# 192 instead of 160 gathered token slots in the last stage of a streaming encoder layer on one core

## What is computed

```
def block(args):
    xb, idb, gb = args
    h = jax.nn.gelu(jnp.einsum('td,thkd->thk', xb, u_table[idb]), approximate=False)
    w = (gb * h).astype(xb.dtype)
    return jnp.einsum('thk,thkd->td', w, v_table[idb]).astype(xb.dtype)
...
x = layer_norm(ALPHA * x + peer(x, peer_w_query, peer_sub_keys, peer_u, peer_v), ln2_g, ln2_b)
```

## Time and profile before

| what | value |
|---|---|
| median of 3 runs | 3592.86 us |
| the profiled execution | 3591.76 us |
| its span | 3590.0 us |
| TensorE (PE) busy | 3506.9 us, 98% |
| VectorE (DVE) busy | 2732.9 us, 76% |
| ScalarE (ACT) busy | 1186.2 us, 33% |
| GpSimd (POOL) busy | 1856.6 us, 52% |
| mean granted TensorE clock | 0.991 of full speed |

### The profile page before, as it was taken

One profiled execution on the slowest core, in us unless ns is written; L12 is line 12 of the kernel. 1 busy time (PEld: TensorE's weight loads), 2 busy tenths in 40 slices (PEclk: granted clock), 3 DMA queues, 4 the chain that ended last, 5 costly groups with the idle time before them and its releaser, 6 DMA issues. The chain is left out here.

```text
span 3590.0 us, 62687 instructions
## 1 busy us (share of the span) xinstructions
PE 3506.9 (98%) x25376; PEld 3461.0 (96%) x25376; DVE 2732.9 (76%) x3476; ACT 1186.2 (33%) x1155; POOL 1856.6 (52%) x1107
## 2 busy tenths in 40 slices
PE   8999999998999999999999999999999999999996
PEld 7999999898999999999999999999999999999996
DVE  4866858634899787777777777776688888888876
ACT  2332333413222234444444434443222222222224
POOL 3443434455444577868887870002665666664321
PEclk9999999999999999999999999999999999999998
DMA  4222222563225678888988897778799999898962
GB/s 153 74 76 77 82 73 71 201 276 132 83 94 165 201 208 228 220 228 226 228 219 229 225 229 217 230 224 288 277 354 351 351 360 361 343 361 351 356 259 99
DMA packets 466252, 788.24 MB, mean 220 GB/s; under 512 B 78976, under 2 KB 376384, under 8 KB 402384
## 3 DMA queue, kind: packets, MB, share of 16 engines
q1 hardware_dynamic: 337920, 547.99, 46.3%
q0 software_dynamic: 83840, 168.15, 14.7%
q10 hardware_dynamic: 44368, 70.57, 5.4%
HBM read 711.43 MB, written 209.34 MB: 256 GB/s over the span
## 5 line engine op out<-in xcount | busy, mean ns | idle before, releaser
L616 POOL TENSOR_TENSOR wl<-wraw,wh 128x512 fp32r<-128x512 f32 x352 | 539.9, 1564 | 686.5 <-ACT wh L1121 678.6
L667 POOL DMA_INDIRECT g_scratch<-picks,g_col x384 | 682.0, 1776 | 175.9 <-issue 149.4
L1121 ACT ACTIVATE wh<-wraw 128x2048 fp32r<-128x2048 f32 x216 | 414.0, 1917 | 970.2 <-PE ps L1037 740.4
L1037 PE MATMUL ps<-Wh,wh 128*128 128x384 f32 x2048 | 686.4, 335 | 7.6 <-DVE wl L2029 3.8
L1037 PE MATMUL ps<-Wh,wl 128*128 128x384 f32 x2048 | 684.8, 334 | 0.0
L1037 PE MATMUL ps<-Wl,wh 128*128 128x384 f32 x2048 | 684.8, 334 | 0.0
L1005 PE MATMUL ps<-xh,wl 128*128 128x272 f32 x1792 | 518.5, 289 | 0.0
L1005 PE MATMUL ps<-xl,wh 128*128 128x272 f32 x1792 | 515.5, 288 | 0.0
L1005 PE MATMUL ps<-xh,wh 128*128 128x272 f32 x1792 | 515.1, 287 | 0.3 <-DVE wl L1914 0.3
L707 PE MATMUL ps<-xh,wh 128*128 128x272 f32 x2304 | 490.1, 294 | 18.3 <-DVE ext L1671 11.9
L707 PE MATMUL ps<-xl,wh 128*128 128x272 f32 x2304 | 481.0, 290 | 0.0
(11 more groups left out here) (311 smaller groups left out, 6886.7 us busy)
## 6 DMA issues: line engine op xcount, KB each, us to landing
wraw<-in_u_t SPq DMA_DIRECT2D x128, 1024.0 KB
v_rows<-in_v_t SPq DMA_DIRECT2D x256, 512.0 KB
wraw<-in_v_t SPq DMA_DIRECT2D x128, 1024.0 KB
wraw<-in_w_in SPq DMA_DIRECT2D x40, 1024.0 KB
g_scratch<-zeros ACTq DMA_DIRECT2D x32, 768.0 KB, 7.7
h_scratch<-hb ACTq DMA_DIRECT2D x64, 384.0 KB
gt<-g_scratch SPq DMA_DIRECT2D x64, 384.0 KB
hg<-h_scratch SPq DMA_DIRECT2D x64, 384.0 KB
```

Source lines behind the costliest of these rows:

```text
L616: ins = nc.gpsimd.tensor_tensor(wl[:, u, part], wraw[:, u, part], f(wh[:, u, part]), ALU.subtract)
L667: nc.gpsimd.indirect_dma_start(g_elem, bass.IndirectOffsetOnAxis(ap=idx, axis=0), gate, None, compute_op=ALU.add).then_inc(g_put, 16)
L1037: ins = mat(out, w[:, u, d * EG + e], m[:, e], start=(begin and e == 0 and w is wh and m is Wh[v]), stop=(end and e == EG - 1 and w is wl))
L1121: go(wh[:, u], wraw[:, u], ACT.Copy).then_inc(whi, 1)
```

## The change

`TD` becomes 352. The dense way then has 352 tokens, and the gathered way 192: the last 128 as before and the 64 tokens 352 to 415, on 128 partitions as two parts of 64 (`NB` = 2), which take 64 slots. `ALL` becomes 192. They are spread over 116 tiles, 3 to 118, instead of 110. The GELU values are gathered 8 slots ahead instead of 32 (`HB`), and the weights are formed for 8 slots at a time. In `v_tile` the two blocks' products with `wh` come first, then both blocks' products with `wl`, and the wait for `wl` stands in front of these. The turning of `y_x` moves from behind tile 118 to behind tiles 120 and 122, in two halves, and its sum is added to `acc` in two halves inside the last group's loop. `fsum1`, `fsum2` and `fsq` move to the memory of the gather buffers.

```diff
-TD = 384
+TD = T - P - RT
-NGC = TD // GC
+NGC = -(-TD // GC)
-NB = P // TS
-XSLOTS = SLOTS // NB
+XSLOTS = -(-SLOTS // NB)
-HB = 32
+HB = 8
...
+RT, NB = 64, 2
...
             def v_tile(g, v, i, u):
 
+                pe.wait_ge(whi, (g * EG + (A_V + u + 1)) + i * 2)
+                pe.wait_ge(w_s, g * (EG // 2) + EG // 2)
+                outs = [v_out(i, u, d) for d in range(2)]
+                for d, (out, kept) in enumerate(outs):
+
+                    pe.wait_ge(y_add, g * KT + (i * 4 + (2 * u + d + 1)))
+                    begin = not kept or (isinstance(g, int) and g == 0)
+                    for e in range(EG):
+                        mat(out, wh[:, u, d * EG + e], Wh[v][:, e], start=(begin and e == 0), stop=False)
+                        mat(out, wh[:, u, d * EG + e], Wl[v][:, e], start=False, stop=False)
                 pe.wait_ge(dlo, (g * EG + (A_V + u + 1 - D0)) + i * 2)
-                pe.wait_ge(w_s, g * (EG // 2) + EG // 2)
-                for d in range(2):
-
-                    pe.wait_ge(y_add, g * KT + (i * 4 + (2 * u + d + 1)))
-                    out, kept = v_out(i, u, d)
+                for d, (out, kept) in enumerate(outs):
+                    end = not kept or (isinstance(g, int) and g == NG - 1)
                     for e in range(EG):
-                        ins = v_products(v, u, d, e, out, not kept or (isinstance(g, int) and g == 0),
-                                         not kept or (isinstance(g, int) and g == NG - 1))
+                        ins = mat(out, wl[:, u, d * EG + e], Wh[v][:, e], start=False, stop=(end and e == EG - 1))
                     ins.then_inc(mm, 1)
...
-                if m == EG - 2:
-                    pe.wait_ge(y_sp_u, 4)
+            for m in range(EG):
+                v_tile(NG - 1, 1, m // 2, m % 2)
+                if m in (0, 2):
+                    half = m // 2
+                    pe.wait_ge(y_sp_u, 4 + half)
                     pe.wait_ge(y_sp_s, 2)
-                    for k in range(KT):
-                        ins = mat(ps[:, TURN, k * TS:(k + 1) * TS], y_x[:, k * P:(k + 1) * P], fold[:],
+                    for j in range(HK):
+                        k = half * HK + j
+                        ins = mat(ps[:, TURN, j * RT:(j + 1) * RT], y_x[:, k * P:(k + 1) * P], fold[:],
                                   start=True, stop=True)
                     ins.then_inc(y_turn, 1)
-            v_group(NG - 1, 1)
...
-            STEP0, STEPS = EG, (NG - 1) * EG - EG - 2
+            STEP0, STEPS = 3, (NG - 1) * EG - 4
...
             for k in range(KT):
+                if k % HK == 0:
+                    v_.wait_ge(y_turn, 5 + k // HK)
+                    a_ = acc[:, k:k + HK, TD:T - P]
+                    C.done(stt_(a_, a_, ALPHA, ps[:, TURN, 0:HK * RT].rearrange("p (k t) -> p k t", k=HK),
+                                ALU.mult, ALU.add), y_sp_u)
                 add_y((NG - 1) * EG + k // 2, k % 2)
```

More of the change, by code:

```diff
@@ L265, in program @@
-        zeros = at("zeros", [P, 4, TD], F32, S0)
[L266 to L271, removed]
+        XB = XSLOTS * 4
+        x_ids, x_hid = [at(n, [P, XSLOTS], U32, S0 + 15520 + k * XB) for k, n in enumerate(("x_ids", "x_hid"))]
@@ L273, in program @@
+        s_ids = at("s_ids", [P, SLOTS], U32, S0 + o + 0 * SLOTS * 4)
+        s_hid = at("s_hid", [P, SLOTS], U32, S0 + o + 1 * SLOTS * 4)
+        s_gate = at("s_gate", [P, SLOTS], F32, S0 + o + 2 * SLOTS * 4)
+        s_h = at("s_h", [P, SLOTS], F32, S0 + o + 3 * SLOTS * 4)
+        s_w = at("s_w", [P, SLOTS], F32, S0 + o + 4 * SLOTS * 4)
+        s_tok = at("s_tok", [P, 1], F32, S0 + o + 5 * SLOTS * 4)
         hb = at("hb", [P, 2, 2, T], F32, M0)
-        Wh = [at(f"Wh{v}", [P, EG, TD], F32R, X0 + v * 2 * EG * ROWD) for v in range(2)]
@@ L275, in program @@
-        Wl = [at(f"Wl{v}", [P, EG, TD], F32R, X0 + v * 2 * EG * ROWD + EG * ROWD) for v in range(2)]
-        G0 = X0 + 4 * EG * ROWD
+        WROW = 384 * 4
+        Wh = [at(f"Wh{v}", [P, EG, 384], F32R, X0 + v * 2 * EG * WROW)[:, :, 0:TD] for v in range(2)]
+        Wl = [at(f"Wl{v}", [P, EG, 384], F32R, X0 + (v * 2 + 1) * EG * WROW)[:, :, 0:TD] for v in range(2)]
+        G0 = X0 + 4 * EG * WROW
         gath = [at(f"gath{v}", [P, D], F32, G0 + v * D * 4) for v in range(3)]
@@ L287, in program @@
         assert (EG + 2) * ROWD <= 15520
-        fsum1 = at("fsum1", [P, T], F32, M0)
-        fsum2 = at("fsum2", [P, T], F32, M0 + ROW)
-        fsq = [at(f"fsq{u}", [P, T], F32, M0 + (2 + u) * ROW) for u in range(2)]
+        fsum1 = at("fsum1", [P, T], F32, G0)
+        fsum2 = at("fsum2", [P, T], F32, G0 + ROW)
+        fsq = [at(f"fsq{u}", [P, T], F32, G0 + (2 + u) * ROW) for u in range(2)]
         XT = HK * TH * 4
@@ L361, in program @@
             sem("slots_done"), sem("slots_turned"), sem("turned_used"))
-        sh_in = [sem(f"slot_h_in{b}") for b in range(ALL // HB)]
+        sh_in = [sem(f"slot_h_in{b}") for b in range(2)]
+        assert ALL % HB == 0 and SLOTS % HB == 0
         sv_in = [sem(f"slot_v_in{b}") for b in range(3)]
@@ L676, in _ @@
                     for tt in G_TILES:
-                        put(g_idx[:, tt, c:c + 1], picks[:, 0, tt, h, k:k + 1])
+                        m = min(P, TD - TOPK_TILES[tt][0])
+                        put(g_idx[0:m, tt, c:c + 1], picks[0:m, 0, tt, h, k:k + 1])
             pool.wait_ge(ids_s, 1)
@@ L1877, in _ @@
             C.done(ts_(s_h[:], s_w[:], float(SD), s_tok[:], ALU.mult, ALU.add), dve)
-            C.done(ts_(s_h[:], s_h[:], float(TS), None, ALU.add), dve)
+            C.done(ts_(s_h[:], s_h[:], float(RT), None, ALU.add), dve)
             C.done(cp(s_hid[:], s_h[:]), dve)
             def rest(a):
-                return picks[0:TS, a, REST].rearrange("p h k -> p (h k)")
+                return picks[0:RT, a, REST].rearrange("p h k -> p (h k)")
             C.done(stt_(r_f[:], rest(1), float(P), rest(2), ALU.mult, ALU.add), dve)
             cp(r_ids[:], r_f[:])
-            C.done(ts_(r_f[:], r_f[:], float(SD), s_tok[0:TS], ALU.mult, ALU.add), dve)
+            C.done(ts_(r_f[:], r_f[:], float(SD), s_tok[0:RT], ALU.mult, ALU.add), dve)
             C.done(cp(r_hid[:], r_f[:]), dve)
[L1888 to L1891, removed]
+            for x in (x_ids, x_hid, x_gate):
+                C.done(nc.vector.memset(x[:], 0), dve)
+            C.done(tt_(fold[:], ident[:, 0:RT], ident[:, RT:2 * RT], ALU.add), ids_s)
             def flat(a):
@@ L2105, in _ @@
                     slot(s)
-            v_.wait_ge(y_turn, 5)
-            a_ = acc[:, :, TD:T - P]
-            C.done(stt_(a_, a_, ALPHA, ps[:, TURN].rearrange("p (k t) -> p k t", k=KT), ALU.mult, ALU.add), dve)
+            v_.wait_ge(slot_s, ALL)
+            v_.sem_inc(y_sp_s, 1)
             nc.vector.memset(fsum1[:], 0.0)
```

42 lines of the change are left out of this document (19 added, 23 removed).

## The result

The changed kernel takes 3572.87 us (median of 5 runs, 3565.95 to 3576.26), the kernel before, on the same chip, 3592.86 us (3589.17 to 3598.6): a ratio of 0.9939, 95% interval 0.9927 to 0.9952. It is faster by 20 us where 46 were forecast. The profiled execution has a span of 3571.1 us, 18.9 less than before.

The account below looks back on a forecast made before the run. VectorE was to become the bound: 62.1 + 1 + 1 = 64.1 us a group. 3591.8 - 44.2 - 5.3 + 2.7 + 1 = 3546, so 3547 us as median; 8-in-10 range 3508 to 3592 us.

Parts of the forecast that it names:

- TensorE's sum: V stage, TensorE's multiplications after the change: 159.5 ns each, 7.66 us a tile, 61.3 us a group.
- VectorE's sum: V stage, VectorE's instructions without waits: 62.1 us a group, above TensorE's 61.3, making VectorE the bound.
- The DMA engines' sum: V stage, moving 3.15 MB a tile: between 60.3 and 65.6 us a group, put at 63.
- The rival of the DMA engines: V stage, transfers bound it at its own mix: 65.6 to 67.5 us a group, 3569 to 3597 us; chance 0.15.
- rival with 353 GB/s as the ceiling: V stage, 353 GB/s is the mix's ceiling: 71.4 us a group, 3654 us; chance 0.03.
- Loss (b): V stage, slots at m = 0 and 1 wait for gathered rows: 1 us a group, bounds 0 and 4.
- Loss (a): V groups, VectorE's uneven work lags beyond what PSUM allows: about 1 us a group lost.
- the lag: V groups, m = 3 to 6: VectorE about 6 us behind; far costlier with `wl` wanted at tile start.
- Gather loop, the slower rival: V stage, three-buffer chain decides; x runs from slot's end to rows three slots later; x = 13.5: 3627 us; chance 0.07.
- The clock's rival: V stage, bunched waits drop TensorE's clock: two drops a group give 68.3 us, 3608 us; chance 0.05.
- The rest: Outside the steady groups: start nothing or 2 us, `y_sp` adds +2.7, `y_x` turning +1, last group -5.3, norm unchanged.
- The 2.7 us for the adds of `y_sp`: Last group but one: VectorE's four adds of turned `y_sp` no longer have slack, +2.7 us.

## Why the prediction was wrong

The direction, the mechanism and the bound were right; the gain was less than half of the forecast, because of one term.

- **TensorE's sum, right.** In the last group the chain shows 16 products with `wl`, 2.56 us, so 160 ns each (forecast 159.5), and a tile every 7.68 us (forecast 7.66):

```profile
3497.69 1.73 PE ps L1115 x16
...
3519.96 2.56 PE ps L1066 x16
3527.64 2.56 PE ps L1066 x16
...
3545.22 4.01 PE ps L769 x16
```

- **VectorE's sum, right**, as the table shows, and VectorE with its waits for rows sets the pace.
- **The DMA engines' sum, right**: 381 GB/s at a share of 0.97, and with four buffers 397 GB/s at 1.00, which makes 3.15 MB x 8 / 397 = 63.5 us a group, where I put 63. They are no bound of the changed kernel, since the same bytes went through in 63.5 us a group once there was a fourth buffer. The rival of the DMA engines (3569 to 3597 us) has the measured time in its range, with the wrong mechanism. But how full they are has a part in how long a gather takes, as the run with half rows shows, without telling it apart from the gather's own bytes. The prediction's rival with 353 GB/s as the ceiling is out as well. The Trainium skill, page "DMA: Bandwidth & Descriptors", section "Where 436 GB/s comes from", says that the HBM side binds at about 358 GB/s, and names in the same place 425 GB/s measured for 16 MB. The 397 GB/s over 762 us of this core speak against the first as a limit of this lone core, and stay below the second.
- **Loss (b), the gather waits: the step that failed.** I took 1 us a group, bounds 0 and 4; measured are 3.5 us. The count of the raw waits was nearly right: four slots of 0 to 2 us, measured 3.2 a group of 1.1 us, three quarters of their time at m = 0 and 1 and most of the rest at m = 2. What failed is the step from there to 1 us, "part falls into the time that VectorE would be ahead anyway". By my own sums VectorE (62.1) is behind TensorE (61.3), and in the changed kernel it waits for TensorE 0.6 us in twelve groups, so there is hardly such time. The fourth buffer shows the cause by taking it away: 3.2 of the 3.5 us vanish, the group falls by 2.6, the kernel by 36 us. The other 0.6 us come back, within 0.9 us of new waits for TensorE and ScalarE; so a small part would have been hidden, not three quarters.
- **The inputs of loss (b) were off both ways, and the right count is half luck.** With the waits themselves taken off, the distances at m = 0 and 1 were 7.8 to 13.5 us, longer than the 7.3 to 9.6 that I counted. And the need was longer than the 10.8 us that I took for its most. That figure bounds only the slots at the shortest distance. In the kernel before, by the packets' records, the rows of 19 of 138 slots landed more than 10.8 us after their buffer was free, up to 14.2 us, unseen because their distances were longer still; in the changed kernel 38 of 159 did, up to 13.2 us, with a mean of 10.2. I had also not counted that GpSimd issues late (at most a quarter of the waits, by the run without value gathers).
- **Loss (a), about right in size, wrong in place.** I took 1 us; beyond 62.1 and the gather waits the changed kernel has 0.5 us a group, the one with four buffers 1.1. I expected TensorE to wait some 3 us a group for `acc`. It waits 3.3 us, for the last `Wl`, a wait that I had not named. It is no loss of its own: with W earlier the same time turns up at `acc`, and the kernel is no faster.
- **The new order**, without which I said the lag would cost far more, is worth about 4 us at most in the changed kernel, hardly clear of the noise. In the kernel before it gives 0.4 us a group, as forecast.
- **Gather loop, the slower rival.** Its mechanism is what happened, but as a lack of distance at some slots, not as a loop that is full on average: at x = 10.2 its formula gives 13.24 / 3 x 12.5 = 55 us a group, under 62.1. A mean over the loop hid what its shortest distances cost.
- **The clock's rival.** Four times in the twelve groups the granted clock fell to 0.50, for 20.5 us in all, each time within or right behind one of TensorE's waits for the last `Wl`. The first, where TensorE had stood still for 5.3 us:

```profile
2607.00:2614.00 7.00, 3.78 (x13) 3.79 (x14) 6.79 (x5) 1.91 (x1) 6.36 (x3) 0.51 0.93 317
```

  It is not the loss: VectorE hardly waits for TensorE, and with W earlier the clock stays at 1.00 while the group is no shorter.
- **The rest.** The turning of `y_x` takes 2 x 1.7 us, less than the 5.5 of the earlier trace rows. The norm at the end is 1.3 us longer: from 3540 to 3550 us the granted clock is 0.66, with TensorE busy 6 of 10 us, and the 16 multiplications of L769 take 4.0 us; before, the ten microseconds behind the last add stood at 1.00, and the same 16 took 2.1 us. The 2.7 us for the adds of `y_sp` were not measured by themselves.

What stays open: how much of the 0.8 to 1.6 us a group that VectorE still waits with four buffers is due to full DMA engines or to the ring of the V tiles, and whether slots at better places could save the waits without memory for a fourth buffer. My one plan for that didn't.

## What to carry to other kernels

When a buffer ring feeds an engine that is to become the bound, compare its shortest distance, not its mean, with the longest time from the freed buffer to the landed data. What is missing is lost for the most part, because an engine at its bound has little slack to hide it: here 2.6 of 3.2 us came back with a fourth buffer, 1.2 of 2.0 with half rows. And a wait that shows on the engine next door (here TensorE for `Wl`) is to be followed to its source before it is mended: moving the late piece only moves the wait. A buffer more is often the cheapest cure: here 8 KB a partition, half of it from W's padding, were worth 36 us, more than the change itself.

## What the hardware showed that I had not expected

- One core's 16 DMA engines carried 397 GB/s for 762 us with a share of 1.00, in a mix of 1 MB tiles, gathers of 8 KB rows and gathers of single values.
- A gather of 128 rows of 4 KB instead of 8 KB took 7.2 us from issue to landing instead of 9.2: halving its bytes, and with them the load, saved 2 us, no more. 4.7 of the 9.2 us (4.2 of the 7.2) had passed before its first packet started.
- GpSimd's issue of one gather took 0.94 to 3.06 us, about 2 on average, and no less when it had half as many to issue (2.0 us each, 325.69 us for 160): what lengthens it wasn't tried.
- With two buffers TensorE was busy 803 of 986 us and its granted clock was 0.93 on average, against 1.00 in the kernel before with the new order, where it was busy 799 of 799. But it also stood at 1.00 with W earlier, busy 755 of 798 us, where its waits were 1.8 us at the longest; in the changed kernel, with waits of up to 5.3 us, it was 0.99.
